# Two-block transformer step on one core: modulation rows moved to the vector engine in 1024-column operations

## The reference

```
# first block
cond = silu(c)
mod = cond @ w_ada[i] + b_ada[i]                       # 2048 x 12288
shift1, scale1, gate1, shift2, scale2, gate2 = split(mod, 6)
h = _modulate(_rms(x, norm1_w), shift1, scale1); ...   # mixer
x = x + gate1 * (concatenate([y_ssm, y_att]) @ w_out)  # output projection
h2 = _modulate(_rms(x, norm2_w), shift2, scale2)
x = x + gate2 * ((silu(h2 @ w_ffn_gate) * (h2 @ w_ffn_up)) @ w_ffn_down)

# second block, layers i = 0, 1
def modulation(cvec, ada_w, ada_b):
    return split(silu(cvec) @ ada_w + ada_b, 3)        # 2048 x 6144 each
sh_l, sc_l, g_l = modulation(c, ada_w[i], ada_b[i])
sh_c, sc_c, g_c = modulation(c_ctx, ada_w[i], ada_b[i])   # layer 0: shift and scale are used
```

## Time and profile before

| | |
|---|---|
| median of three runs | 2645.53 us |
| profiled execution | 2646.84 us, span 2645.1 us |
| PE busy | 2471.7 us (93%) |
| DVE busy | 1640.3 us (62%) |
| ACT busy | 1035.2 us (39%) |
| granted TensorE clock, mean | 0.966 |
| chain that ended last | PE 84%, DVE 5%, POOL 3%, DMA 3% |
| moved by DMA | 589.43 MB, mean 223 GB/s |

### The profile page before, as it was taken

How to read it: one execution, slowest core, us unless ns; L and a number is a source line. 1 busy time by engine, 2 the same in 40 slices (tenths; PEclk the granted TensorE clock), 3 DMA queues, 4 the chain that set the end, 5 groups by cost and what they waited for, 6 DMA issues and landing times.

```text
span 2645.1 us, 37763 instructions
## 1 busy us (share of the span) xinstructions
PE 2471.7 (93%) x15318; PEld 2074.8 (78%) x15318; DVE 1640.3 (62%) x1973; ACT 1035.2 (39%) x1370; POOL 217.2 (8%) x193
## 2 busy tenths in 40 slices
PE   5898887989999999999999999999887999999995
PEld 2587765559888888989887887777677899999994
DVE  8654634456777788785676565443565585765557
ACT  2443753224333333333333454444332433334331
POOL 0146800001000000000011000000002000000000
PEclk9899988999999999999999999999898999999998
DMA  9853458987999999997553753323354675665451
GB/s 390 303 170 120 127 210 313 370 300 248 347 351 345 357 359 348 343 332 253 155 168 122 236 157 101 98 91 119 127 184 144 196 247 179 225 229 180 154 176 40
DMA packets 278061, 589.43 MB, mean 223 GB/s; under 512 B 20608, under 2 KB 29824, under 8 KB 276608
## 3 DMA queue, kind: packets, MB, share of 16 engines
q1 hardware_dynamic: 277888, 587.02, 64.6%
HBM read 584.85 MB, written 2.10 MB: 222 GB/s over the span
## 4 chain that ended last, share of the span: by engine, by line
PE 84%; DVE 5%; POOL 3%; DMA 3%; ACT 2%; issue 2%; SPq 0%; DVEq 0%; ACTq 0%; POOLq 0%
PE psum L206 13%; PE psum L208 13%; PE psum L207 13%; PE psum L218 11%; PE psum L220 11%; PE psum L219 11%; PE psum L278 3%; DMA start_slots<-in_w_ada 2%; POOL pool_scan_tmp L779 1%; PE psum L2355 1%; PE psum L1744 1%; DVE wlo L195 1%; PE psum L2329 1%; PE psum L2330 1%; POOL xacc L779 1%
## 5 line engine op out<-in xcount | busy, mean ns | idle before, releaser
L195 DVE TENSOR_TENSOR wlo<-raw,whi 128x1024 fp32r<-128x1024 f32 (+2 forms) x728 | 881.9, 1229 | 672.6 <-ACT whi L189 666.5
L189 ACT CAST whi<-raw 128x1024 fp32r<-128x1024 f32 (+2 forms) x728 | 738.0, 1024 | 976.7 <-PE psum L208 429.1
L218 PE MATMUL psum<-hh,whi 128*128 128x256 f32 x2432 | 685.8, 282 | 4.4 <-DVE wlo L195 4.4
L219 PE MATMUL psum<-hh,wlo 128*128 128x256 f32 x2432 | 679.1, 279 | 0.0
L220 PE MATMUL psum<-hl,whi 128*128 128x256 f32 x2432 | 679.1, 279 | 0.0
L218 PEld LDWEIGHTS psum<-hh,whi 128*128 128x128 f32 x2432 | 459.3, 189 | 26.8 <-issue 25.9
L220 PEld LDWEIGHTS psum<-hl,whi 128*128 128x128 f32 x2432 | 462.4, 190 | 0.0
L219 PEld LDWEIGHTS psum<-hh,wlo 128*128 128x128 f32 x2432 | 458.5, 189 | 1.3 <-issue 1.0
L206 PE MATMUL psum<-whi,hh 128*128 128x512 f32 (+1 forms) x864 | 354.2, 410 | 29.1 <-DVE wlo L195 25.3
L208 PE MATMUL psum<-whi,hl 128*128 128x512 f32 (+1 forms) x864 | 341.2, 395 | 0.0
L207 PE MATMUL psum<-wlo,hh 128*128 128x512 f32 (+1 forms) x864 | 340.6, 394 | 0.0
(11 more groups left out here) (349 smaller groups left out, 2270.9 us busy)
## 6 DMA issues: line engine op xcount, KB each, us to landing
araw<-in_ada_w SPq DMA_DIRECT2D x128, 512.0 KB, 6.4
raw<-in_w_in_fourier SPq DMA_DIRECT2D x128, 512.0 KB, 4.0
raw<-in_w_ffn_gate SPq DMA_DIRECT2D x88, 512.0 KB, 10.8
raw<-in_w_ffn_up SPq DMA_DIRECT2D x88, 512.0 KB, 7.4
raw<-in_w_ffn_down SPq DMA_DIRECT2D x88, 512.0 KB, 10.8
raw<-in_w_in_attn SPq DMA_DIRECT2D x88, 512.0 KB, 4.3
araw<-in_w_ada SPq DMA_DIRECT2D x80, 512.0 KB, 6.6
start_slots<-in_w_ada SPq DMA_DIRECT2D x64, 512.0 KB, 8.2
```

What stands on the lines that cost most here:

```text
L189: nc.scalar.copy(whi[:, u % SPLITS, 0:kn, 0:w], raw[:, u % RING, 0:kn, 0:w]).then_inc(s_hi, 1)
L195: nc.vector.tensor_tensor(wlo[:, u % SPLITS, 0:kn, 0:w], raw[:, u % RING, 0:kn, 0:w], whi[:, u % SPLITS, 0:kn, 0:w].bitcast(F32), ALU.subt ...
L218: nc.tensor.matmul(o, h, hh[:, kt + k], start=(kt + k == 0 and f % 2 == 0), stop=False)
L219: nc.tensor.matmul(o, lw, hh[:, kt + k], start=False, stop=False)
```

## The change

16 of the 112 rounds leave PE. Pair 9 of the first block (q = 18 and 19) is summed on DVE in the output projection, and pair 15 of the second block, which serves two condition vectors, in steps 1 to 8 of the feed-forward layer (`dual_load`, `dual_sum`, `dual_reduce`, `dual_store`). Every sum on DVE is now made in operations of 1024 columns over both q of a pair, and `ada_load` loads 128 whole rows of 1024 columns for each of them. `araw` now belongs to the sums from the middle of the output projection on, and the slots of the rounds from number 56 on have the 4 parts of `kt4` only. Rounds 52 to 71 stand behind units n = 0 to 19 on PE as before; the slots of rounds 52 to 55 are loaded behind the raw loads of n = 0 to 3, and those of rounds 56 to 71 behind the raw loads of n = 9 to 24.

```
-    PE_PAIRS = (0, 1, 2, 3, 4, 5, 6, 7, 8, 9, 12, 13, 14, 15)
-    PE_SETS = ((0, 4, 1), (4, 2, 1), (6, 4, 1), (10, 4, 2))
+    PE_PAIRS = (0, 1, 2, 3, 4, 5, 6, 7, 8, 12, 13, 14)
+    PE_SETS = ((0, 4, 1), (4, 2, 1), (6, 3, 1), (9, 3, 2))
...
+            if 8 <= m < 64 or 72 <= m < 112:
+                sp.wait_ge(s_aused, (m - 8) // 2 + 1)
+            elif 112 <= m < 144:
+                sp.wait_ge(s_aused, (m - 4) // 2 + 1)
...
+    def ada_load(sp, q, kt):
+        w, c = ada_src(q)
+        n = 16 * pair_rank(q) + kt
+        if n < 4:
+            sp.wait_ge(s_aused, 53 + n // 2)
+        else:
+            sp.wait_ge(s_acc, n - 3)
+        sp.dma_start(arawf[:, 1024 * (kt % 4):1024 * (kt % 4) + 1024],
+                     w[kt * P:(kt + 1) * P, c:c + 2 * CW]).then_inc(s_slot[kt % 4], 16)
...
+    def ada_sum(dve, q, kt):
+        g = pair_rank(q)
+        if kt == 0 and g:
+            dve.wait_ge(s_red, g)
+        dve.wait_ge(s_slot[kt % 4], 16 * (SLOT_USES[2] + 4 * g + kt // 4 + 1))
...
+            ins = nc.vector.scalar_tensor_tensor(out=acc, in0=w, scalar=s, in1=acc, op0=ALU.mult, op1=ALU.add)
+        ins.then_inc(s_acc, 1)
...
+    def dual_sum(dve, kt):
+        w, landed, count = ffn_slot(kt // 2, 6 + kt % 2)
+        dve.wait_ge(landed, count)
...
+        for v in range(2):
...
+                ins = nc.vector.scalar_tensor_tensor(out=acc2[:, v], in0=w, scalar=s, in1=acc2[:, v],
+                                                     op0=ALU.mult, op1=ALU.add)
+        ins.then_inc(s_dual, 1)
+    def dual_reduce(pe):
...
+        for v in range(2):
+            for j in range(8):
+                ins = nc.tensor.matmul(psum[:, 6, 8 * v + j:8 * v + j + 1], acc2[:, v, j * P:(j + 1) * P], ones[:, 0:1],
+                                       start=True, stop=True)
...
@@ pairs_dve, behind low of unit j @@
+                if u0 == U_OUT and 0 <= 16 * (i or 0) + j - 11 < 16:
+                    ada_sum(dve, 18, 16 * (i or 0) + j - 11)
...
@@ out_sp, behind the raw load of unit n @@
-            if n < 28:
+            if n < 4:
                 slots_sp(sp, 104 + 2 * n, 106 + 2 * n)
+            if 9 <= n < 25:
+                slots_sp(sp, 94 + 2 * n, 96 + 2 * n)
+            if 8 <= n < 24:
+                ada_load(sp, 18, n - 8)
...
@@ out_pe, behind the multiply of unit n @@
-            if n < 28:
+            if n < 20:
                 rounds_pe(pe, 52 + n, 53 + n)
+            if n == 29:
+                ada_reduce(pe, 18, 5)
...
@@ hidden_sp @@
-            if not H.fourier and 1 <= c <= 8 and j % 3 == 2:
-                slots_sp(sp, 160 + 8 * (c - 1) + j // 3, 160 + 8 * (c - 1) + j // 3 + 1)
+            if not H.fourier and 1 <= c <= 8:
+                if j % 3 == 2 and j < 18:
+                    slots_sp(sp, 144 + 6 * (c - 1) + j // 3, 144 + 6 * (c - 1) + j // 3 + 1)
+                if j in (20, 23):
+                    dual_load(sp, 2 * (c - 1) + (j - 20) // 3)
...
@@ hidden_dve, then hidden_pe @@
+            if not H.fourier and not first and c <= 8 and j in (18, 20):
+                dual_sum(dve, 2 * (c - 1) + (j - 18) // 2)
-            if not H.fourier and 1 <= c <= 8 and j % 6 == 5:
+            if not H.fourier and 1 <= c <= 8 and j in (5, 11, 17):
```

More of the change, by code:

```diff
@@ L340, in program @@
[L340 to L356, removed]
@@ L362, in ada_reduce @@
+    def ada_reduce(pe, q, bank=6):
+        g = pair_rank(q)
+        pe.wait_ge(s_acc, 16 * (g + 1))
         if g:
             pe.wait_ge(s_mod, g)
-        for c in range(2):
-            for j in range(4):
-                ins = nc.tensor.matmul(psum[:, 6, 4 * c + j:4 * c + j + 1], acc[:, c, j * P:(j + 1) * P], ones[:, 0:1],
-                                       start=True, stop=True)
[L368 to L372, removed]
-        nc.vector.tensor_tensor(modc[:, 4 * q:4 * q + 8], psum[:, 6, 0:8], bias, ALU.add).then_inc(s_mod, 2)
+        for j in range(8):
+            ins = nc.tensor.matmul(psum[:, bank, j:j + 1], acc[:, j * P:(j + 1) * P], ones[:, 0:1], start=True, stop=True)
+        ins.then_inc(s_red, 1)
@@ new lines, in ada_store, with dual_load @@
+    def ada_store(dve, q, bank=6):
+        dve.wait_ge(s_red, pair_rank(q) + 1)
+        bias = cols[:, COLS["bada"].start + 4 * q:COLS["bada"].start + 4 * q + 8]
+        nc.vector.tensor_tensor(modc[:, 4 * q:4 * q + 8], psum[:, bank, 0:8], bias, ALU.add).then_inc(s_mod, 1)
+    s_dual, s_dred = sem("two_vector_ops"), sem("two_vector_reduced")
+    def dual_load(sp, kt):
+        t, landed, _ = ffn_slot(kt // 2, 6 + kt % 2)
+        sp.wait_ge(s_aused, R_FFN + 3 * (kt // 2) + 2)
+        sp.dma_start(t, dram["ada_w_2"][0][kt * P:(kt + 1) * P, 3 * 1024:4 * 1024]).then_inc(landed, 16)
@@ new lines, in dual_reduce, with dual_store @@
+    def dual_reduce(pe):
+        pe.wait_ge(s_dual, 16)
+        pe.wait_ge(s_mod, 9)
+        for v in range(2):
+            for j in range(8):
+                ins = nc.tensor.matmul(psum[:, 6, 8 * v + j:8 * v + j + 1], acc2[:, v, j * P:(j + 1) * P], ones[:, 0:1],
+                                       start=True, stop=True)
+        ins.then_inc(s_dred, 1)
+    def dual_store(dve):
+        dve.wait_ge(s_dred, 1)
+        bias = cols[:, COLS["bada"].start + 120:COLS["bada"].start + 128]
+        nc.vector.tensor_tensor(modc[:, 120:128], psum[:, 6, 0:8], bias, ALU.add)
+        nc.vector.tensor_tensor(modx[:, 24:32], psum[:, 6, 8:16], bias, ALU.add)
@@ L1677, in hidden_dve @@
                 first_turn_dve(dve, H, j, j + 1)
-            pos = ADA24 if n == 24 else ADA_AFTER
-            if q is not None and j in pos:
-                a = pos.index(j)
-                ada_sum(dve, q + a // 4, a % 4)
+            if q is not None and j in ADA24:
+                for kt in range(2 * ADA24.index(j), 2 * ADA24.index(j) + 2):
+                    ada_sum(dve, q, kt)
+            if not H.fourier and not first and c <= 8 and j in (18, 20):
+                dual_sum(dve, 2 * (c - 1) + (j - 18) // 2)
         if H.fourier and first:
@@ L1812, in hidden_pe @@
                     set_turn_pe(pe, 3)
+                    dual_reduce(pe)
                 if j in (11, 13, 17, 19):
@@ L1820, in hidden_pe @@
                 ctx_turn_pe(pe, j // 2 - 1)
-            if q is not None and j == (13 if first else 19):
+            if q is not None and j == 19:
                 ada_reduce(pe, q)
```

90 lines of the change are left out of this document (52 added, 38 removed).

## The result

The changed kernel takes 2712.6 us (2710.9 to 2714.3, 4 runs), the kernel before in the same session 2646.6 (2645.4 to 2648.8, 4 runs): a ratio of 1.0248, 95% interval 1.0231 to 1.0266. It is slower, as forecast, but by 66 us where 49 were forecast, and it lies just outside the range of 2668 to 2712. Its profiled execution took 2713.2 us, with a span of 2711.5.

A forecast was written before the change was run, and what follows sets the result against it. PE's own work was taken as the bound. From 2646.84 us: -13.3 PE work, +50.2 stalls, +14 clock made 2697.7; 2696.4 against the median, put at 2695 for vanishing small stalls. Range holding 8 in 10: 2668 to 2712.

The forecast's parts named there:

- The mechanism and its places: Output projection: from k = 8 slots wait behind sum loads, one unit of lead for four; stalls sum to 50.2 us.
- The first part of the turn: Output projection, from unit k-1's end: cast and low part 2.4 us, sum 1.3; block taken out at k = 8, 16: 3.72.
- A fourth 524,288 bytes at 401 GB/s are 1.31 us: 7.6 us.: Output projection, four loads ahead of a round: 6.3 us for three into an empty queue, plus 1.31, make 7.6 us.
- The fixed part of a load: Loads ahead of rounds: 2.0 us fixed by the skill, 2.4 by the rows; each turn would be 0.4 us shorter.
- The clock: Output projection: PE at 1.2 GHz behind six stalls of 6 us and more, 2.3 us each, 14 us; bounds 0 to 17.
- Rival 1: Output projection: stalls come, but the clock does not fall or small stalls hide it; 2682 us, chance 22%.
- my own formula: Output projection: stall(k) = 11.3 - 3.95 - stall(k-1), so two neighbouring rounds have 7.35 us between them.
- PE's own work in the output projection: 8 rounds less, -9.2 us, and one more `ada_reduce`, +1.7 us.
- The feed-forward layer: Feed-forward steps 1 to 8 on PE: 8 rounds less, -9.2 us, and `dual_reduce`, +3.4 us.
- DVE in the feed-forward layer: DVE stays under 60 of some 71.5 us a step, may run some 8 us behind unnoticed; costed at 0.
- rival 4: Feed-forward layer: DVE becomes the bound, +16 to +24 us on top of the forecast; 2711 to 2719 us, chance 13%.
- The bounds: Output projection: turn 10.5 to 12.3 us, giving stalls of 44 to 57 us; whole kernel 2668 to 2712 us.

The follow-up runs named there:

- the run with the slots first: Changed kernel with a round's two slots issued ahead of the raw load of their place in SP's order, not behind it: 2697.9 us, 1.0180 of the kernel before.
- the kernel with two units of lead: Changed kernel with the slots of rounds 56 to 71 loaded behind the raw load of unit k+2, not k+5: 2667.8 us, 1.0067 of the kernel before.
- the one with batches apart: Changed kernel with sum loads of odd kt from 5 on held until the round of the batch before is done: 2711.5 us, 1.0241 of the kernel before.

## Why the prediction was too low, step by step

- **The mechanism and its places: right.** The slots are held by the sum loads, six long pauses of 8.8 to 11.5 us at rounds 8, 10, 12, 14, 16 and 18 behind PE's units, the first at 493 us, none in between after unit 7. Moving the sums alone took the loss from 66 us to 5.
- **The first part of the turn: right.** Sum 1.28 us (1.3 put); the block taken out ahead of the low part stands in the chain at k = 8 and again at k = 16 (pauses of 10.9 and 11.5 us).
- **The step that failed: "A fourth 524,288 bytes at 401 GB/s are 1.31 us: 7.6 us."** The four loads took 9.4 us. The fourth load was priced with the rate of a full queue, but this queue was empty at each turn, and the weight unit was in second place. Its removal from the path gave 2.9 us. This is 1.8 us in each of six turns, 10.8 us: stalls of 59.1 us for 48.9 (50.2 less 1.3, for which see the clock below). The 6.3 us for three loads stood beside a measured 6.5, but in part by luck: the three of the earlier trace rows were two slots and a weight unit in third place, the three of the run with the slots first were all of 4 KB rows.
- **The fixed part of a load.** The 2.0 us that the prediction takes from the Trainium skill, "DMA: Bandwidth & Descriptors", section "Anatomy of one DMA — SWDGE (gpsimd) path", are given there for loads that GpSimd issues; SP issues those here. The first load of a batch landed 3.6 to 4.0 us after its issue, 2.5 in the mean over its 1.31, so no turn was shorter by that figure.
- **The clock: right in size.** 13.2 us for 14. Rival 1, without this term, is out: the low level was there behind all six pauses. The small stalls beside the slow units vanished, as I had put when I went from 2696.4 to 2695. By my own formula the long stall of a pair then grows by what the small one loses, so that only 1.3 us of the 50.2 go.
- **PE's own work in the output projection: 1.6 us missed.** The reduction took 1.68 us as put, but it stands next to the turn of the set, 3.5 us of small matmuls together, and the next two units took 7.34 us, where the kernel before has 5.76. The granted clock was 0.50 from 642.5 to 645.9 us, and the chain shows it. The small matmuls do not always bring it: in the kernel with two units of lead and in the one with batches apart the same two groups stand side by side, and the two units behind them took 5.76 us.

```profile
637.95 1.68 PE psum L380 x16
639.63 1.79 PE psum L320 x16
641.42 0.34 PE psum L206
...
642.76 0.43 PE psum L208
643.18 0.43 PE psum L206
```

- **The feed-forward layer: -2.7 us for -5.8.** The double reduction took 4.71 us for 3.4 (behind its middle, from 1301.2 to 1308.1 us, the granted clock was 0.50). Seven steps from reduction to reduction gave 7.4 us, when a round each by the earlier trace rows would be 8.1 and the eight 9.2. A step went from 72.63 to 72.04 only: a round is gone, 1.1 us, but the 381 gaps between neighbouring matmuls of 256 columns sum to 44.07 us, for 43.56 before. In the two last steps before they summed to 45.19 (74.26 and 74.25 us a step), and those two give 2.2 each. What sets this spacing was not found. The chain has the double reduction:

```profile
1299.06 4.71 PE psum L415 x32
```

- **DVE in the feed-forward layer costed at nothing: right, and rival 4 is out,** though its 2711 to 2719 us hold the time. DVE is busy for 59.5 of 72.05 us in the step, and PE for all of them. That the right total stood beside a wrong reason is chance: the missing us were in the output projection.
- **The rest,** 2.5 us, is before and behind these two stages (the first unit starts 1.2 us later; 1.3 us behind the feed-forward layer). The profiled executions of all kernels here start that unit anywhere from 447.8 to 453.4 us, so it is not put down to the change. Together: 10.3 us for the stalls (the loads, less 0.5), 1.8 for PE's own work in the output projection (1.6 of it in those two units), 3.1 for the feed-forward layer, 2.5 for the rest, less 0.8 for the clock make 16.9 us between the profiled executions; the medians, 2712.6 and a forecast of 2695, are 17.6 apart.
- **The bounds were too narrow.** For the turn I gave 10.5 to 12.3 us, as if a load's price were known from the other state of the queue; from the end of unit k-1 to the restart it measured 12.8 to 13.5 (k = 10, 12, 14 and 18). The stalls, 44 to 57 by those bounds, were 59.1, and the total left the stated range by 0.6 us.

## What to carry to other kernels

Ask what wait stands ahead of a load in its queue's program, not only when its own buffer comes free: here the slots lost their lead to a neighbour's wait for another engine, and that cost some 60 us. Price a batch of loads in the state of the queue in which it will be issued, and by its order (in an empty queue, with a reader waiting, the weight unit in second place cost 2.9 us and not 1.31), and put what is waited for first in it. Before taking work from an engine in a stage whose DMA queue is full as well, count the bytes: in the runs here the gain ended at the queue.

## What the runs showed of the chip that I had not expected

- Between otherwise equal feed-forward steps of one execution, 256-column matmuls follow each other every 114.3 or every 118.6 ns (43.56 and 45.19 us over 381), and at 115.6 or 115.7 ns in each step of the changed kernel, all at a granted clock of 1.00 in the table by stretches. It moves a step by up to 1.6 us.
- Behind the pauses of 8.8 to 11.5 us the level of 1.2 GHz held for stretches of 6.8 to 13.6 us, which reach into the pause: two of them here, two above.

```profile
495.70:509.30 13.60, 4.94 (x15) 2.72 (x16) 1.45 (x2) 0.00 (x0) 0.00 (x0) 0.50 0.88 309
...
540.10:546.90 6.80, 3.05 (x11) 1.23 (x12) 0.00 (x0) 0.00 (x0) 0.00 (x0) 0.50 1.02 395
```

- A second batch of four loads, begun 2.3 to 4.0 us behind the first, held it up by 0.6 us only (9.4 for 8.8 us), as if the queue had served them nearly in order.
